# The last round of a feed-forward layer reordered on VectorE, small loads spread between weight loads, and square and root taken tile by tile

## The reference, cut to what matters

```
x = layer_norm(ALPHA * x + 0.5 * swiglu(x, ffn1...), ln_g[0], ln_b[0])
y = concat(pool_mixer, gated_conv_mixer, neighbourhood_attention)(x @ w_in) @ w_out
x = layer_norm(ALPHA * x + y, ln_g[1], ln_b[1])
x = layer_norm(ALPHA * x + 0.5 * swiglu(x, ffn2...), ln_g[2], ln_b[2])
```

```
x = x + 0.5 * rmsnorm(swiglu(rmsnorm(x, ng[0]), w_ffn_in[0], w_ffn_out[0]), ng[1])
x = x + rmsnorm(mixer(rmsnorm(x, ng[2])), ng[3])
x = x + rmsnorm(mem_attn(rmsnorm(x, ng[4]), rmsnorm(mem)), ng[5])
x = x + 0.5 * rmsnorm(swiglu(rmsnorm(x, ng[6]), w_ffn_in[1], w_ffn_out[1]), ng[7])
```

## Time and profile before

| | |
|---|---|
| median of 3 runs | 3088.74 us (3088.4 to 3089.52) |
| profiled execution | 3089.14 us, span of its instructions 3087.2 us |
| mean granted TensorE clock | 0.939 |
| busy: TensorE | 2788.6 us (90%) |
| busy: VectorE | 1583.1 us (51%) |
| busy: ScalarE | 1287.9 us (42%) |
| busy: GpSimd | 477.0 us (15%) |
| read from memory | 441.99 MB, 144 GB/s over the span |

### The profile page before, as it was taken

How to read it: one execution, slowest core, us unless ns; L and a number is a source line. 1 busy time by engine, 2 the same in 40 slices (tenths; PEclk the granted TensorE clock), 3 DMA queues, 4 the chain that set the end, 5 groups by cost and what they waited for, 6 DMA issues and landing times.

```text
span 3087.2 us, 52843 instructions
## 1 busy us (share of the span) xinstructions
PE 2788.6 (90%) x21412; PEld 2564.5 (83%) x21412; DVE 1583.1 (51%) x2182; ACT 1287.9 (42%) x1830; POOL 477.0 (15%) x199
## 2 busy tenths in 40 slices
PE   7989899898989989888889898998988888989898
PEld 7978798797879879777779787987977777978898
DVE  5566555555655555532555525555553254552555
ACT  3435444343544434434523444444443452344443
POOL 0000000000000000033424650000003342465000
PEclk9989999898999989898999998998989899999999
DMA  7665465566446546532322544655652232254464
GB/s 233 184 163 157 123 185 175 171 183 164 151 125 188 170 148 186 166 94 82 94 72 70 184 130 136 184 163 155 186 165 89 82 103 63 78 183 123 143 184 129
DMA packets 622823, 445.06 MB, mean 144 GB/s; under 512 B 27904, under 2 KB 589344, under 8 KB 622176
## 3 DMA queue, kind: packets, MB, share of 16 engines
q1 hardware_dynamic: 622688, 443.09, 47.8%
HBM read 441.99 MB, written 1.05 MB: 144 GB/s over the span
## 4 chain that ended last, share of the span: by engine, by line
PE 85%; DVE 9%; ACT 3%; issue 1%; DMA 1%; POOL 0%; SPq 0%; DVEq 0%; ACTq 0%; POOLq 0%
PE ps L357 18%; PE ps L358 17%; PE ps L359 17%; PE ps L373 7%; PE ps L374 7%; PE ps L375 6%; PE ps L583 2%; PE ps L607 1%; PE ps L400 1%; PE ps L1365 1%; ACT w_hi L624 1%; PE ps L1172 1%; PE ps L1079 1%; PE ps L1355 1%; DVE zT L1507 1%
## 5 line engine op out<-in xcount | busy, mean ns | idle before, releaser
L357 PE MATMUL ps<-in_hi,w_hi 128*128 128x256 f32 x4352 | 1266.8, 291 | 63.9 <-POOL w_lo L818 31.0
L358 PE MATMUL ps<-in_lo,w_hi 128*128 128x256 f32 x4352 | 1252.2, 288 | 0.0
L359 PE MATMUL ps<-in_hi,w_lo 128*128 128x256 f32 x4352 | 1250.8, 287 | 0.0
L624 ACT ACTIVATE w_hi<-raw 128x1024 fp32r<-128x1024 f32 x788 | 832.2, 1057 | 964.0 <-PE ps L359 632.8
L818 DVE TENSOR_TENSOR w_lo<-raw,w_hi 128x1024 fp32r<-128x1024 f32 x594 | 727.9, 1225 | 761.2 <-ACT w_hi L624 760.4
L357 PEld LDWEIGHTS ps<-in_hi,w_hi 128*128 128x128 f32 x4352 | 857.3, 197 | 85.9 <-issue 34.1
L358 PEld LDWEIGHTS ps<-in_lo,w_hi 128*128 128x128 f32 x4352 | 857.4, 197 | 7.1 <-issue 0.5
L359 PEld LDWEIGHTS ps<-in_hi,w_lo 128*128 128x128 f32 x4352 | 856.0, 197 | 0.0
L818 POOL TENSOR_TENSOR w_lo<-raw,w_hi 128x1024 fp32r<-128x1024 f32 x194 | 476.5, 2464 | 2357.4 <-ACT w_hi L624 2356.5
L373 PE MATMUL ps<-w_hi,hid_hi 128*128 128x512 f32 x704 | 283.3, 402 | 31.6 <-DVE hid_lo L892 31.6
L374 PE MATMUL ps<-w_lo,hid_hi 128*128 128x512 f32 x704 | 282.1, 401 | 0.0
(11 more groups left out here) (301 smaller groups left out, 2694.9 us busy)
## 6 DMA issues: line engine op xcount, KB each, us to landing
raw<-in_w_ffn_in SPq DMA_DIRECT2D x176, 512.0 KB, 3.7
raw<-in_w_mix SPq DMA_DIRECT2D x112, 512.0 KB, 3.6
raw<-in_ffn_w_gate SPq DMA_DIRECT2D x88, 512.0 KB, 3.7
raw<-in_ffn_w_up SPq DMA_DIRECT2D x88, 512.0 KB, 3.7
raw<-in_ffn_w_down SPq DMA_DIRECT2D x88, 512.0 KB, 3.5
raw<-in_w_ffn_out SPq DMA_DIRECT2D x88, 512.0 KB, 3.5
raw<-in_w_in SPq DMA_DIRECT2D x40, 512.0 KB, 4.7
raw<-in_w_out SPq DMA_DIRECT2D x32, 512.0 KB, 3.6
```

The source lines that it names most:

```text
L357: nc.tensor.matmul(o, lh, rh, start=first, stop=False, **kw)
L358: nc.tensor.matmul(o, lh, rl, start=False, stop=False, **kw)
L359: return nc.tensor.matmul(o, ll, rh, start=False, stop=last, **kw)
L624: nc.scalar.activation(w_hi[:, e % SPLIT, :], raw[:, e % RAW, :], ACT.Copy).then_inc(sem("split_high"), 1)
```

## The change

1. On VectorE the gated tile of tile 21 is made at `after(63)`, ahead of the low halves of pieces 66 and 67, instead of behind them.
2. In `act_square_sum` the root of a tile follows its square at once; the second tile's square comes behind the first tile's root.
3. In three of the feed-forward rounds' load programs (first round of the first block, both of the second) SyncE's inner loop is unrolled and calls `between(t)` behind the loads of tile `t`. The small loads are issued there: `vec1` and `pool_w` at tile 2, one `rpb` load per tile from tile 3 to 18, a gain or bias at tiles 4, 6, 8 and 10, `post_gain[0]` and `post_gain[3]` at tile 5 of their rounds. `post_gain[1]` goes ahead of the memory's key and value weights, `post_gain[2]` behind them. Each of the four has a semaphore of its own.

```diff
@@ sp_ffn
+            if between is not None:
+                for j in range(TILES):
+                    tile(j)
+                    between(j)
+            else:
+                for j in range(4):
+                    tile(j)
+                with sp.Fori(0, TILES // 2 - 2) as it:
+                    tile(4, it)
+                    tile(5, it)
@@ dve_ffn, after
+                if e == FFN_PIECES - 3:
+
+                    hidden(TILES - 1, it)
                 if e < FFN_PIECES - 1 and e0 + e + SPLIT < end:
                     low_part(dve, e0 + e + SPLIT, it)
                 elif e < FFN_PIECES - 1 and tail is not None:
                     tail(e0 + e + SPLIT - end)
-                if up is None and whole is not None:
+                if up is None and whole is not None and e != FFN_PIECES - 2:
                     hidden(whole, it)
@@ act_square_sum
                 ready(t)
                 nc.scalar.activation(squares[:, t, :], src(t), ACT.Square, accum_out=square_sum[:, t:t + 1])\
                     .then_inc(sem("tok_stat"), 1)
-            for t in range(HALF):
                 act.wait_ge(sem("tok_stat"), HALF * n + t + 1)
@@ VectorE's second block: post_here becomes post_here0 to post_here3
-                dve.wait_ge(sem("post_here"), 16)
+                dve.wait_ge(sem("post_here0"), 16)
@@ SyncE, layer1
-                for n in range(2):
-                    across(ln_gain[n], a["ln_gb"][l, n, 0], "ln_here")
-                    across(ln_bias[n], a["ln_gb"][l, n, 1], "ln_here")
-                sp_ffn(sp, E1_FFN1, *ffn1(l))
+                def between(t):
+
+                    if t == 2:
+                        sp.dma_start(vec1[:, :], a["vec1"][l]).then_inc(sem("vec_here"), 16)
+                        sp.wait_ge(sem_pw, 1)
+                        for g in range(4):
...
+                    if 3 <= t < 3 + 2 * NA_HEADS:
+                        half, h = divmod(t - 3, NA_HEADS)
...
+                    if t in (4, 8):
+                        across(ln_gain[t // 4 - 1], a["ln_gb"][l, t // 4 - 1, 0], "ln_here")
+                    if t in (6, 10):
+                        across(ln_bias[t // 4 - 1], a["ln_gb"][l, t // 4 - 1, 1], "ln_here")
+
+                sp_ffn(sp, E1_FFN1, *ffn1(l), between=between)
@@ SyncE, layer2
-                across(post_gain[0], a["norm_post"][l, 0], "post_here")
-                sp_ffn(sp, E_FFN1, *ffn2(l, 0))
+                sp_ffn(sp, E_FFN1, *ffn2(l, 0),
+                       between=lambda t: t != 5 or across(post_gain[0], a["norm_post"][l, 0], "post_here0"))
...
-                for r in range(1, 4):
-                    across(post_gain[r], a["norm_post"][l, r], "post_here")
+                across(post_gain[1], a["norm_post"][l, 1], "post_here1")
                 sp_linear(sp, E_KV, columns(wkv[l], 8, range(4, 8)))
+                across(post_gain[2], a["norm_post"][l, 2], "post_here2")
```

More of the change, by code:

```diff
@@ L328, in sp_first, with sp_ffn @@
                     sp.dma_start(ident, a["const"][:, 0:P]).then_inc(ident_here, 16)
-        def sp_ffn(sp, e0, w_gate, w_up, w_down):
+        def sp_ffn(sp, e0, w_gate, w_up, w_down, between=None):
             def tile(j, it=0):
@@ L1972, in layer2 @@
                 dve_rms(dve, steps, 0, mem_n, lambda k: col2("mem_norm", k), mem_n, C_KV, "mem_ready")
-                dve.wait_ge(sem("post_here"), 4 * 16)
+                dve.wait_ge(sem("post_here1"), 16)
                 dve_post(dve, steps, 3, 1, post_gain[1])
@@ L1982, in layer2 @@
                     low_part(dve, e)
+                dve.wait_ge(sem("post_here2"), 16)
                 dve_post(dve, steps, 5, 2, post_gain[2])
@@ L1988, in layer2 @@
                         None if last else lambda i: low_first(dve, l + 1 + LAYERS, order2, [i]))
+                dve.wait_ge(sem("post_here3"), 16)
                 dve_post(dve, steps, 7, 3, post_gain[3])
@@ L2070, in layer1 @@
             def layer1(l, following):
-                for n in range(2):
-                    across(ln_gain[n], a["ln_gb"][l, n, 0], "ln_here")
-                    across(ln_bias[n], a["ln_gb"][l, n, 1], "ln_here")
-                sp_ffn(sp, E1_FFN1, *ffn1(l))
[L2076 to L2085, removed]
+                def between(t):
[3 more added lines that the diff above has]
+                        for g in range(4):
+                            o = 64 * (g % 2)
+                            sp.dma_start(pool_w[o:o + 64, g // 2, o:o + 64], a["pool_w"][l][g])\
+                                .then_inc(sem("pool_w_here"), 16)
+                    if 3 <= t < 3 + 2 * NA_HEADS:
+                        half, h = divmod(t - 3, NA_HEADS)
                         row = a["rpb"][l][h]
@@ L2122, in layer2 @@
                 sp_linear(sp, E_OUT, rows(w_out2[l]))
-                for r in range(1, 4):
-                    across(post_gain[r], a["norm_post"][l, r], "post_here")
+                across(post_gain[1], a["norm_post"][l, 1], "post_here1")
                 sp_linear(sp, E_KV, columns(wkv[l], 8, range(4, 8)))
+                across(post_gain[2], a["norm_post"][l, 2], "post_here2")
                 sp_linear(sp, E_Q, columns(wq[l], 4))
                 sp_linear(sp, E_O, rows(wo[l]))
-                sp_ffn(sp, E_FFN2, *ffn2(l, 1))
+                sp_ffn(sp, E_FFN2, *ffn2(l, 1),
+                       between=lambda t: t != 5 or across(post_gain[3], a["norm_post"][l, 3], "post_here3"))
                 if following is not None:
```

## The result

The changed kernel takes 3038.82 us, the median of 4 runs (3037.72 to 3042.81), against 3088.57 us for the kernel before beside it (4 runs, 3081.03 to 3089.52). The ratio is 0.9846, with a 95% interval from 0.983 to 0.9862. The profiled execution took 3038.53 us with a span of 3036.6, so 50.6 us went out of the span where 42.7 were forecast. The mean granted clock is 0.951.

What follows compares the result with a forecast made beforehand. TensorE was taken to bound the kernel, gaining only where it idles or runs slowly. Ends and starts gave 40.7 us, 42.7 with the jumps: span 3087.2 to 3044.5, median 3046.0 us, range 3040 to 3055.

Steps and rivals of the forecast that it cites:

- Part 1, gated tile: Round ends: TensorE goes on without a gap; 4.1 us each at three second-block ends, 3.0 each at first-block second-round ends.
- Part 2, root by root: Norms: first root fills a gap; 1.3 us at three norms behind rounds, 1.4 at four ahead of stages.
- The table: no cost: ScalarE's norms: alternating squares and roots brings no table load between them, so a cost of 0 was taken.
- the strict reading of the prediction: ScalarE's norms: a table switch with each root, two more 1.28 us loads at ten calls, 26 us, 3072; chance 0.02.
- Part 3, small loads: SyncE's queue: pieces of `w_in` no longer 2.6 us late at the first end; cost taken 0, bounds 0 and 22 us.
- Part 4, the jumps: TensorE's two loop jumps: issue stalls of 3.62 and 3.22 us could stay or vanish (6.8 us); 2 us taken.
- rival 1: TensorE's loop jumps: the stalls stay, giving 3048 us; chance 0.2.
- the sign "shorter or equal": TensorE's loop jumps: "issue" there would be no longer than before, 3.62 and 3.22 us.
- rival 3: Stage starts: transposes and first matmuls stay longer at low clock, 1 us at ten starts costs 5, 3051 us; chance 0.08.

Runs made afterwards that it cites:

- table_gap: The changed kernel with the square root's table load moved into ScalarE's gap ahead of the split of piece 67: 3040.18 us, ratio to before 0.984.
- pool_low: The changed kernel with GpSimd making the low half of piece 67 at the first block's four ends: 3038.54 us, ratio to before 0.9833.
- loads_only: The kernel before with only the small loads moved, gated tile and root order as before: 3084.57 us, ratio 0.9986.
- late_last: The changed kernel with five memsets on VectorE ahead of the norm starting the last round, both layers: 3049.27 us against 3044.44 for the changed kernel.
- gated_only: The kernel before with only the gated tile moved ahead of the low halves: 3057.98 us against 3088.99, ratio 0.9903.

## Why the prediction was right, and where it was not

- **Part 1, gated tile: right.** No wait for `hid_lo`, 5.04 us at the first block's ends (forecast 5.14), 5.29 at the second's (5.3). table_gap and pool_low confirm what was named as late next at each: taking it away moved that norm and no other.
- **Part 2, root by root: right in its place, and too small in its effect.** The waits of 1.33 and 1.47 us are 0 and 0.43 us. At both last-round starts the transposes gained 1.37 us against 1.4. What this started was not in the sum; see the last point.
- **The table: no cost, right.** ScalarE: Activation LUTs of the Trainium skill, "Table sets: the hidden batching unit", has activations batched by table set, and by the strict reading of the prediction each call here would get two more loads; the rows show squares and roots alternating with no ACT_TABLE_LOAD between, and 47 loads in the trace before and after. The section's exception for cheap functions would fit that, though it doesn't name the square.
- **Part 3, small loads: right.** ScalarE's waits for `w_in` are gone, loads_only shows 2.6 and 3.5 us at the two ends where 2.6 and 3.1 were forecast, and no load of weights became late.
- **Part 4, the jumps: its 2 us didn't come.** The stalls are 3.87 and 4.03 us, where they were 3.62 and 3.22; rival 1 was right, and the sign "shorter or equal" didn't come either. In all thirteen profiles the first is 3.60 to 4.15, with or without traffic, and an instruction packet falls into it. The Trainium skill's Runtime: NRT & Kernel Launch, "Instruction fetch mechanics", says that a jump to a target outside the window waits for a DMA fetch; that agrees with this packet. The second ranges from 2.38 to 4.03 and falls to 0.69 and 0.74 only with quiet DMA engines. Removing one load of `post_gain[0]` left the traffic as it was: just ahead of that stall the DMA engines moved 282 GB/s before and 289 after. The prediction had named this, other weight loads that follow at once, as its reason for taking little.
- **The failed step: "they run there at low clock today too, so no change is my case" (rival 3).** Parts 1 to 3 gave about 41.4 us for 40.7. The clock gave some 10.3 us for 0. The rival saw the right place but the wrong sign: it priced a longer stay at half speed, not a shorter one, although the trace before has each start of the second block at 1.2 GHz for some 9 us. late_last shows that at the last rounds the moment of the start decides: 4.0 us at low clock in every profile with the new order and no delay, 8.9 to 9.5 in every other, and a delay brings it back. Why just these moments, the runs don't tell: in late_last the idle time ahead and the moment moved together, and gated_only has both outcomes behind equal idle times. In the span, 50.6 for 42.7, the errors are +10.3 for the clock, +0.7 for parts 1 to 3 and -3.1 for part 4; that the total missed by no more than 7.9 is partly luck, for they have opposite signs. The Trainium skill says, in TensorE: Matmul & The Clock Gate, Part 1, that the same kernel can stay cold for different stretches from run to run; the spells in the mixers do that here, the last-round starts didn't.
- **The three parts alone give 31.0 + 22.6 + 4.4 = 58.0 us, together 45 to 50.** The places add up: 24.9 us in the distances of gated_only, 6.1 in those of loads_only and the 10.7 of the roots are 41.7, against 41.4 together. The clock's share doesn't. That an early rise at a start can be gained only once, and that each part shifts the later starts, would explain it, but isn't shown.

## What to carry to other kernels

At the end of a stage, first find the one operation on which the bound engine waits and put all work for later stages behind it; then ask what is late next at each kind of end, since it can be another engine (ScalarE's table load here, VectorE's low half there), and each is worth an edit of its own. Before costing a start at "no change", look at the granted clock behind it: at each last round a start 1.4 us earlier was worth another 2.3 us, and one 1.95 us later cost another 2.0. A stall of "issue" at a loop's jump is worth a test with quiet DMA queues before it is blamed on loads or on the jump; here the stall at one of two was the jump's own and the other came mostly from loads.

## What the runs showed of the hardware

- The time at 1.2 GHz behind a stage's first transpose was 2.8 to 9.5 us at starts of the second block without a jump in them, and up to 11.2 us (the kernel before, 2092.94) at the one with a jump.
- Executions of one and the same kernel (the changed one) went from 3037.72 to 3046.75 us, and the mean granted clock of its profiled ones from 0.951 to 0.946: a spread of 0.3%. Matched matmul by matmul, most of the 8.1 us between the two profiled ones lies in stretches that ran at 1.2 GHz in one and at 2.4 in the other.
- After a jump TensorE can issue part of the work (11 transposes) and then lack instructions for 2.4 to 4.0 us, 0.7 if the DMA engines are quiet. In both cases it goes on 2.6 to 2.7 us behind the start of a 16 KB instruction packet; the loads delay that start, 4.03 us behind the first transpose instead of 0.60.
